# A feed forward gate through logarithm, exponential and a Newton step, and four down weights split earlier

## What is computed

```
ab = einsum('btd,df->btf', h, w_up)
a, gate_in = ab[..., :D_FF], ab[..., D_FF:]
ext = concatenate([prefix, a], axis=1)
conv = conv_b
for tap in range(3):
    conv = conv + ext[:, tap:tap + T] * conv_w[tap]
y = einsum('btf,fd->btd', jax.nn.silu(conv) * gate_in, w_down)
```

## Time and profile before

| | us |
|---|---|
| median of 3 runs | 2005.04 (2001.98 to 2007.12) |
| the profiled execution, its own time | 2003.92 |
| its span | 2002.1 |
| TensorE busy | 1887.2 (94%) |
| VectorE busy | 1269.0 (63%) |
| ScalarE busy | 519.5 (26%) |
| GpSimd busy | 524.3 (26%) |
| mean granted TensorE clock | 0.978 of full speed |

### The profile page before, as it was taken

One profiled execution on the slowest core, in us unless ns is written; L12 is line 12 of the kernel. 1 busy time (PEld: TensorE's weight loads), 2 busy tenths in 40 slices (PEclk: granted clock), 3 DMA queues, 4 the chain that ended last, 5 costly groups with the idle time before them and its releaser, 6 DMA issues.

```text
span 2002.1 us, 34856 instructions
## 1 busy us (share of the span) xinstructions
PE 1887.2 (94%) x15062; PEld 1614.6 (81%) x15062; DVE 1269.0 (63%) x1579; ACT 519.5 (26%) x918; POOL 524.3 (26%) x384
## 2 busy tenths in 40 slices
PE   7999999998899799989998789899999999999999
PEld 7988888884566344449997579899999999999998
DVE  5485674665676887875333636885488187386585
ACT  5222221353543354552121422000010000000006
POOL 2211221240000234422234013222323332332340
PEclk8999999998999899999999979999999999999999
DMA  7211211132000788853024302111211211211212
GB/s 233 53 44 33 55 49 28 44 80 97 1 1 31 273 326 325 328 187 116 23 85 147 116 17 59 41 46 40 57 49 34 63 43 32 64 38 37 64 43 88
DMA packets 161142, 174.64 MB, mean 87 GB/s; under 512 B 21847, under 2 KB 146797, under 8 KB 156605
## 3 DMA queue, kind: packets, MB, share of 16 engines
q1 hardware_dynamic: 145072, 91.43, 15.7%
q0 software_dynamic: 7168, 75.50, 10.0%
q10 hardware_dynamic: 8750, 5.49, 0.9%
HBM read 159.24 MB, written 13.25 MB: 86 GB/s over the span
## 4 chain that ended last, share of the span: by engine, by line
PE 72%; DVE 20%; ACT 4%; issue 3%; DMA 1%; POOL 0%; ACTq 0%; DVEq 0%; POOLq 0%; SPq 0%
PE PS L748 16%; PE PS L750 15%; PE PS L749 15%; DVE cu L2318 4%; PE PS L1033 4%; PE PS L785 4%; PE PS L1066 3%; DVE ct L2302 2%; PE PS L980 2%; PE PS L829 2%; PE PS L958 2%; PE PS L1023 2%; PE PS L1048 1%; DVE Sst L1891 1%; DVE atail L2306 1%
## 5 line engine op out<-in xcount | busy, mean ns | idle before, releaser
L694 POOL CAST whi<-wraw 128x1024 fp32r<-128x1024 f32 (+4 forms) x142 | 136.3, 960 | 1054.2 <-PE PS L750 932.6
L748 PE MATMUL PS<-BH,whi 128*128 128x344 f32 x1152 | 370.1, 321 | 6.2 <-DVE cu L1823 6.2
L749 PE MATMUL PS<-BL,whi 128*128 128x344 f32 x1152 | 367.9, 319 | 0.0
L750 PE MATMUL PS<-BH,wlo 128*128 128x344 f32 x1152 | 367.8, 319 | 0.0
L696 POOL TENSOR_TENSOR wlo<-wraw,whi 128x1024 fp32r<-128x1024 f32 (+4 forms) x142 | 289.8, 2041 | 11.4
L748 PEld LDWEIGHTS PS<-BH,whi 128*128 128x128 f32 x1152 | 217.0, 188 | 6.9 <-DVE cu L1823 6.4
L749 PEld LDWEIGHTS PS<-BL,whi 128*128 128x128 f32 x1152 | 217.1, 188 | 0.5 <-issue 0.5
L750 PEld LDWEIGHTS PS<-BH,wlo 128*128 128x128 f32 x1152 | 216.9, 188 | 0.0
L748 PE MATMUL PS<-XH,whi 128*128 128x344 f32 x528 | 179.9, 341 | 3.1 <-DVE XL L1778 3.1
L2221 DVE TENSOR_TENSOR XT<-PS,XT 128x1032 f32<-128x1032 f32 x48 | 59.2, 1233 | 179.7 <-PE PS L750 179.6
L749 PE MATMUL PS<-XL,whi 128*128 128x344 f32 x528 | 169.2, 320 | 0.0
(11 more groups left out here) (443 smaller groups left out, 3692.5 us busy)
## 6 DMA issues: line engine op xcount, KB each, us to landing
wraw<-in_w_up_dram SPq DMA_DIRECT2D x44, 512.0 KB, 3.9
wraw<-in_w_in_dram SPq DMA_DIRECT2D x20, 512.0 KB, 4.0
wraw<-in_w_down_dram SPq DMA_DIRECT2D x24, 256.0 KB, 2.8
wraw<-in_w_down_dram SPq DMA_DIRECT2D x16, 320.0 KB, 3.2
xt_kept<-XT SPq DMA_DIRECT2D x1, 4128.0 KB, 12.7
XT<-xt_kept SPq DMA_DIRECT2D x1, 4128.0 KB, 13.8
xstage<-in_x_prompt_dram SPq DMA_DIRECT2D x8, 512.0 KB, 10.3
wraw<-in_w_out_dram SPq DMA_DIRECT2D x8, 512.0 KB, 4.5
```

The costliest lines, as they stand in the source:

```text
L694: gp.tensor_copy(hi, raw).then_inc(w_hi_done, 1)
L748: pe.matmul(out, wh[:, t, 0:m], hi[:, tile(t), s], start=(t == first), stop=False)
L749: pe.matmul(out, wh[:, t, 0:m], low, start=False, stop=False)
L750: ins = pe.matmul(out, wl[:, t, 0:m], hi[:, tile(t), s], start=False, stop=(t == last))
```

## The change

Two things. The jobs of down(4, 0) to down(4, 3) are put into the list behind a19, b19, a20 and b20, one each; ring places are now counted over the jobs that use the ring. So SyncE's loads and GpSimd's splits of these four come there. And in the gate ScalarE goes on after the exponential e: s = exp(-ln(e + 1)), an approximate 1/(1 + e), into SQ. VectorE then makes one Newton step and the product: (e + 1) s, then (that - 2) s, which is the negative reciprocal, then (-ct) times that. XMIN goes from -87 to -43.

```diff
--- before.py
+++ after.py
@@ -43,7 +43,7 @@
 NF = FF // P
 CW = 3
 EPS = 1e-6
-XMIN = -87.0
+XMIN = -43.0
 EMAX = 4e18
 SCALE = float(QK) ** -0.5
 MSCALE = float(P) ** -0.5
@@ -243,7 +243,7 @@
         m_max, m_new, om_hi = sem("m_max"), sem("m_new"), sem("om_hi")
         sk_in, sv_in = [sem(f"sk_in{n}") for n in range(2)], sem("sv_in")
         qs_set, prod_done, s_max, s_exp, s_new2 = sem("qs_set"), sem("prod_done"), sem("s_max"), sem("s_exp"), sem("s_new2")
-        ab_new, conv_new, conv_exp, act_new, act_hi, act_lo = [sem(n) for n in ("ab_new", "conv_new", "conv_exp", "act_new", "act_hi", "act_lo")]
+        ab_new, conv_new, conv_exp, conv_seed, act_new, act_hi, act_lo = [sem(n) for n in ("ab_new", "conv_new", "conv_exp", "conv_seed", "act_new", "act_hi", "act_lo")]
         tail_out = sem("tail_out")
         end_sq, end_ss, end_xg = sem("end_sq"), sem("end_ss"), sem("end_xg")
         y_out = [sem(f"y_out{n}") for n in range(4)]
@@ -354,34 +354,40 @@
                 for c in range(KD):
                     yield "down", (n, c)
 
+        last = len(FPARTS) - 1
+
+        def down_job(n, c):
+            f0, f1 = FPARTS[n][0], FPARTS[n][-1] + 1
+            job(("down", n, c), f1 - f0, [(0, cols(w_down[f0 * P:f1 * P], c * P, c * P + P))])
+
         for kind, what in ffn_order():
             if kind == "up":
-                job(("a", what), KD, [(0, cols(w_up, what * P, what * P + P))])
-                job(("b", what), KD, [(0, cols(w_up, FF + what * P, FF + what * P + P))])
-            else:
-                n, c = what
-                f0, f1 = FPARTS[n][0], FPARTS[n][-1] + 1
-                job(("down", n, c), f1 - f0, [(0, cols(w_down[f0 * P:f1 * P], c * P, c * P + P))])
-
-        def wtile(ring, j):
-            k = jobs[j][1]
-            return ring[j % 2][:, 0:k * P].rearrange("p (k m) -> p k m", k=k)
-
-        last = len(FPARTS) - 1
+                for m, name in enumerate(("a", "b")):
+                    job((name, what), KD, [(0, cols(w_up, m * FF + what * P, m * FF + what * P + P))])
+                    if what in (NF - 3, NF - 2):
+                        down_job(last, 2 * (what - NF + 3) + m)
+            elif what[0] < last or what[1] >= 4:
+                down_job(*what)
 
         def in_last(name):
             return name[0] == "down" and name[1] == last
 
+        ring_jobs = [j for j in range(len(jobs)) if not in_last(jobs[j][0])]
+        ring_place = {j: n for n, j in enumerate(ring_jobs)}
+
+        def wtile(ring, at_, k):
+            return ring[at_ % 2][:, 0:k * P].rearrange("p (k m) -> p k m", k=k)
+
         def weights(j):
 
-            name = jobs[j][0]
+            name, k = jobs[j][0], jobs[j][1]
             if in_last(name):
                 c = name[2]
                 if c < 4:
                     return lasth[c][:, :, :], lastl[c][:, :, :]
-                home, part = (job_no[("a", NF - 1)] + (c - 4) // 2) % 2, slice(512 * (c % 2), 512 * (c % 2) + 512)
+                home, part = (ring_place[job_no[("a", NF - 1)]] + (c - 4) // 2) % 2, slice(512 * (c % 2), 512 * (c % 2) + 512)
                 return tuple(ring[home][:, part].rearrange("p (k m) -> p k m", k=4) for ring in (whi, wlo))
-            return wtile(whi, j), wtile(wlo, j)
+            return wtile(whi, ring_place[j], k), wtile(wlo, ring_place[j], k)
 
 
         hi_before, ss_before, a_, b_ = {}, {}, 0, 0
@@ -573,7 +579,7 @@
                 full(sp, ("go", GT - 2))
             for c0, src in jobs[j][2]:
                 m = src.shape[-1]
-                sp.dma_start(wtile(wraw, j)[:, :, c0:c0 + m], src).then_inc(w_in_sem[j % 2], 16)
+                sp.dma_start(wtile(wraw, j, jobs[j][1])[:, :, c0:c0 + m], src).then_inc(w_in_sem[j % 2], 16)
 
         w_count = []
         for j in range(len(jobs)):
@@ -688,9 +694,9 @@
                 name = jobs[j][0]
                 if in_last(name):
                     full(gp, ("down", last - 1, KD - 1) if name[2] < 4 else ("ab"[(name[2] - 4) // 2], NF - 1))
-                elif j >= 2:
-                    full(gp, jobs[j - 2][0])
-                (hi, lo), raw = weights(j), wtile(wraw, j)
+                elif ring_place[j] >= 2:
+                    full(gp, jobs[ring_jobs[ring_place[j] - 2]][0])
+                (hi, lo), raw = weights(j), wtile(wraw, j, k)
                 gp.tensor_copy(hi, raw).then_inc(w_hi_done, 1)
                 gp.wait_ge(w_hi_done, j + 1)
                 gp.tensor_tensor(lo, raw, hi, ALU.subtract).then_inc(w_split, 1)
@@ -1652,6 +1658,9 @@
             for f in range(NF):
                 act.wait_ge(conv_new, f + 1)
                 act.activation(cu[:, :], cu[:, :], ACT.Exp, scale=-1.0).then_inc(conv_exp, 1)
+                act.wait_ge(conv_exp, f + 1)
+                step(act.activation(SQ[:, :], cu[:, :], ACT.Ln, bias=ones[:, 0:1]))
+                act.activation(SQ[:, :], SQ[:, :], ACT.Exp, scale=-1.0).then_inc(conv_seed, 1)
                 act.wait_ge(act_new, f + 1)
                 act.activation(acth[:, f % FSLOTS, :], ct[:, :], ACT.Copy).then_inc(act_hi, 1)
 
@@ -2313,10 +2322,10 @@
                 ve.tensor_scalar(cu[:, :], ct[:, :], XMIN, None, ALU.max).then_inc(conv_new, 1)
                 if f == 0:
                     scaled(("b", f), RB2[:, :], RB1[:, :])
-                ve.wait_ge(conv_exp, f + 1)
-                step(ve.tensor_scalar(cu[:, :], cu[:, :], 1.0, None, ALU.add))
-                step(ve.reciprocal(cu[:, :], cu[:, :]))
-                step(ve.tensor_tensor(ct[:, :], ct[:, :], cu[:, :], ALU.mult))
+                ve.wait_ge(conv_seed, f + 1)
+                step(ve.scalar_tensor_tensor(out=cu[:, :], in0=cu[:, :], scalar=1.0, in1=SQ[:, :], op0=ALU.add, op1=ALU.mult))
+                step(ve.scalar_tensor_tensor(out=cu[:, :], in0=cu[:, :], scalar=2.0, in1=SQ[:, :], op0=ALU.subtract, op1=ALU.mult))
+                step(ve.scalar_tensor_tensor(out=ct[:, :], in0=ct[:, :], scalar=-1.0, in1=cu[:, :], op0=ALU.mult, op1=ALU.mult))
                 if f:
                     scaled(("b", f), cu[:, :], RB1[:, :])
                 ve.tensor_tensor(ct[:, :], ct[:, :], cu[:, :] if f else RB2[:, :], ALU.mult).then_inc(act_new, 1)
```

## The result

The median went from 2005.36 us (4 runs) to 1992.05 (1989.02 to 1994.42, 4 runs), a ratio of **0.9938, interval 0.9923 to 0.9954**. Two more timed comparisons gave 0.9942 (0.9926 to 0.9959) and 0.9952 (0.9936 to 0.9968). The forecast was 1999.5 us, range 1995.8 to 2003.5: a gain of 5.5 us against the median then known, 2005.04, where 13.3 was measured.

A forecast was written before the change was run, and what follows sets the result against it. TensorE, busy 94%, was taken as the bound, so only its waits for VectorE's gate could pay: 1.1 + 1.2 + 1.0 + 1.6 = 4.9 us, giving 1999.5 us, range 1995.8 to 2003.5.

The forecast's parts named there:

- three places: TensorE's gate waits: second residual column of down passes 2 and 3 (1.1, 1.2 us), sixth column of last pass (2.3).
- everything there is to win: Feed forward: three gate waits of 1.1, 1.2 and 2.3 us plus 1.65 of slow matmuls, 6.3 us in all.
- The gate's cost in a settled tile: Tile 11: b read 0.7 us later through turns with GpSimd; undisturbed, the chain would be 2.5 us shorter.
- Rival (A): No turn-taking with GpSimd: all three waits and the slow stretch go, 6.3 us, 1997.6 us; chance 0.27.
- Places one and two: Second residual column of down passes 2 and 3 (tiles 14, 18): waits go, -1.1 and -1.2, 0.8 us to spare.
- Place three: Sixth column of the last pass, tile 21: a wait of 1.3 stays of 2.3, -1.0; slow stretch also goes, -1.65.
- The term of the turns: Tile 21: the three new VectorE operations take turns with GpSimd's last two splits, leaving a wait of 1.3 us.
- 1.65: Slow matmuls behind the last pass's pause, TensorE partly at 1.2 GHz: expected to go, bounds 0 and -1.65 us.
- (B): Clock stays down behind the last pause, a 1 to 2 us wait kept: gain 1 to 3.3 us; chance 0.19.
- The moved splits: Four down-weight splits moved earlier: no weight wait changes; at tile 21 columns 4 and 5 done 4 us sooner.
- (C): ScalarE reloads tables between exponential and logarithm: two loads a tile add 2.6 us; chance 0.02, joins (D).
- (D): Slower: disturbance per tile exceeds what the copy to atail absorbs, 2005 to 2007 or up to 2070; chance 0.07, (C) included.

The follow-up runs named there:

- before_early_b: The kernel before, reciprocal and splits unmoved, with every tile's b banks read early, right behind the maximum: ratio 1.0109, feed forward 783.23 us.
- after_early_b: The changed kernel with every tile's b banks read early, right behind the maximum: ratio 0.9949, feed forward 751.62 us.
- gate_only: The kernel before with only the new gate and XMIN, the four splits not moved: ratio 0.9963, feed forward 753.17 us.
- weights_only: The kernel before with only the four splits moved, the reciprocal kept: ratio 0.9986, feed forward 757.75 us.

## Why the prediction was wrong, step by step

**"In the whole feed forward (1370 us to the end) TensorE waits for the gate in three places": wrong.** VectorE's first read of the feed forward stands at 1241.55 us; 1370, from the description of the kernel before, is near the first down pass. The wait of 6.2 us at tile 2, larger than the other three together, was left out of "everything there is to win". The change took 3.1 us off there. The wait also sits in the tiles where VectorE is farthest behind, which the settled tile 11 says nothing about.

**The gate's cost in a settled tile: right.** 0.7 us longer was forecast by turns, 0.2 measured, and not 2.5 shorter. The Trainium skill's rule (SBUF — State Buffer, "SBUF: two separate sides") agrees with these rows: the second operation took 3.32 us beside the subtraction, where the third took 1.23 behind it, and the subtraction grew by 0.86, about what the first operation had left (1.01). Rival (A) fell, although the time it gave lay nearer. Of the three operations that the change removed, two can lose time beside GpSimd as well (the product took 1.97 at tile 0 of the kernel before, add 1 2.92 in before_early_b), so it isn't simply one operation outside the rule for three inside.

**Places one and two: right**, 1.03 and 1.08 us against 1.1 and 1.2, but narrowly. At tile 14 the read ended at 1679.56 and TensorE went on at 1679.77, where 0.8 us were to spare: the three operations lost 1.3 us in turns instead of 0.6.

**Place three: the mechanism right, the size not.** "A wait of 1.3 stays" was wrong; it went altogether, and 3.7 us came back instead of 2.65. The term of the turns was mis-sized: 3.1 us against 1.4, because the first operation was ready 0.5 us sooner after TensorE's event than I had it, and so got ahead of the subtraction. The slow matmuls went with the wait, so 1.65 was right. (B) fell there. At tile 2, where 3.7 us of waiting stayed, slow matmuls stayed too.

**The moved splits: mechanism as forecast, worth more alone** (2.8 to 3.6 us, from the wait and the slow matmuls behind it), and 1.5 us on top of the new gate. No wait for weights or loads appeared. (C) and (D) fell: ScalarE's three operations of 1.07, 1.16 and 1.07 us follow each other within 0.03, so nothing is loaded between them.

**The sum.** 4.9 forecast; 3.1 were missing at tile 2 and 1.1 at place three; with 0.2 less at places one and two that makes the 9.0 us of the feed forward. The remaining 4.3 us of the difference of medians are not explained by the change: they lie in the front and in scatter. Of the later ratios 0.9952 is 9.6 us, which the feed forward accounts for, and 0.9942 is 11.6.

## What to carry to other kernels

List the bound engine's waits over the whole stage and find where the stage starts in the code and in the trace; the first tiles, where a follower engine starts late, can hold more than all the settled ones. Before making a chain cheaper, look at what its operations share with another engine: here the length of GpSimd's *single instructions* counted about as much as the gate's arithmetic. Cutting one of 2.4 us into four took 6.5 us more off the feed forward of the changed kernel, the new gate 7.4 to 8.1; in the kernel before the pieces moved the feed forward by nothing clear of its scatter. Freeing a buffer early by putting a wait into an in-order queue moved the wait here, and with the reciprocal it multiplied it.

## What was not expected of the hardware

- Small operations can be the costliest: two 8-column taps, 0.48 us alone, took 3.48 at tile 0, the time of the rest of a cast and a whole subtraction.
- Not only operations with two inputs take turns: add 1 with one input (0.70 us) took 2.92 beside a subtraction, as the 10-column copy had taken 2.32 in the earlier trace rows. The reciprocal (6.60 us in all 22 tiles of the kernel before) and the reads of the a and b banks (1.22 to 1.23 in both kernels) never did.
- Two engines that are both paced by TensorE can lock in phase: in after_early_b VectorE stayed 8 us behind from tile 1 to tile 4, three periods of 22.56 us, though a tile less its 5.7 us of losses is some 17 us.
- TensorE's pauses of 0.7 to 1.0 us (gate_only, weights_only, the kernel before) were not followed by slow matmuls; those of 2.2 to 6.2 us were. Behind the 1.4 us pause near the end the granted clock was low as well (0.60 from 1980 to 1984 in the kernel after), in a stretch of transposes. In the three that I counted out (tile 2 before and after, place three before) the slow stretch took 4.3 to 4.7 us and added 1.6 to 2.2 us to the pause itself.
